# Key norms of the RWKV-7 recurrence: from 512 columns of head sums to 8 columns with tokens on partitions, spread by products with the identity

## The reference, cut to what matters

```python
kk = heads(k * lp["rwkv_k_k"].astype(f32))
kk = kk / jnp.maximum(jnp.sqrt(jnp.sum(kk * kk, axis=-1, keepdims=True)), 1e-12)
...
y, s = wkv_scan(rh, heads(decay), kh, vh, -kk, kk * ah, s0.astype(f32))
```

## Time and profile before

| | us |
|---|---|
| median of 3 runs (1955.46 to 1959.11) | 1958.74 |
| the profiled execution | 1956.71 |
| its span | 1954.9 |
| PE busy in it | 1886.3 (96%) |
| DVE busy | 1355.1 (69%) |
| ACT busy | 872.5 (45%) |
| PE's share of the chain that ended last | 74% |
| DVE's share of that chain | 15% |

### The profile page before, as it was taken

How to read it: one execution, slowest core, us unless ns; L and a number is a source line. 1 busy time by engine, 2 the same in 40 slices (tenths; PEclk the granted TensorE clock), 3 DMA queues, 4 the chain that set the end, 5 groups by cost and what they waited for, 6 DMA issues and landing times.

```text
span 1954.9 us, 53598 instructions
## 1 busy us (share of the span) xinstructions
PE 1886.3 (96%) x22088; PEld 1748.8 (89%) x22088; DVE 1355.1 (69%) x2232; ACT 872.5 (45%) x1710; POOL 72.2 (4%) x143
## 2 busy tenths in 40 slices
PE   7999999998999999999999999999989999999997
PEld 7999888776789999999999998887667999999997
DVE  3485767888646999962265767688886389999423
ACT  4223335554445566552232234545536355666421
POOL 0000000000000111100000000000000001111000
PEclk9999899999999999999999999999999999999999
DMA  6225534244421333233332264432442222332232
GB/s 223 87 86 157 162 110 141 68 113 115 114 93 55 119 109 100 85 98 98 103 134 87 76 189 149 135 120 68 123 134 86 91 97 88 99 108 87 88 97 91
DMA packets 153014, 214.30 MB, mean 110 GB/s; under 512 B 18497, under 2 KB 118338, under 8 KB 151362
## 3 DMA queue, kind: packets, MB, share of 16 engines
q1 hardware_dynamic: 134050, 200.38, 33.0%
q10 hardware_dynamic: 18720, 10.49, 1.8%
HBM read 202.58 MB, written 16.59 MB: 112 GB/s over the span
## 4 chain that ended last, share of the span: by engine, by line
PE 74%; DVE 15%; ACT 4%; issue 3%; DMA 2%; ACTq 1%; SPq 0%; DVEq 0%
PE ps L1110 12%; PE ps L1112 11%; PE ps L1111 11%; PE ps L1646 5%; PE ps L1648 5%; PE ps L1647 5%; PE ps L1500 4%; PE ps L1378 1%; DMA ring<-in_w 1%; PE ps L1471 1%; PE ps L1367 1%; PE ps L1131 1%; PE ps L1464 1%; PE ps L1132 1%; DVE arena L2500 1%
## 5 line engine op out<-in xcount | busy, mean ns | idle before, releaser
L2226 DVE TENSOR_TENSOR ring_lo<-ring,ring_hi 128x1024 fp32r<-128x1024 f32 x84 | 102.9, 1225 | 196.9 <-ACT ring_hi L1703 195.0
L1112 PE MATMUL ps<-hf_hi,ring_lo 128*128 128x260 f32 x704 | 198.9, 283 | 0.0
L1112 PE MATMUL ps<-in_hi,ring_lo 128*128 128x260 f32 x704 | 198.8, 282 | 0.0
L1703 ACT ACTIVATE ring_hi<-ring 128x1024 fp32r<-128x1024 f32 x84 | 88.8, 1058 | 212.1 <-DMA ring<-in_w 209.6
L1112 PE MATMUL ps<-hm_hi,ring_lo 128*128 128x260 f32 x480 | 136.9, 285 | 0.0
L1112 PEld LDWEIGHTS ps<-hf_hi,ring_lo 128*128 128x128 f32 x704 | 132.7, 188 | 0.0
L1112 PEld LDWEIGHTS ps<-in_hi,ring_lo 128*128 128x128 f32 x704 | 132.6, 188 | 0.0
L1110 PE MATMUL ps<-in_hi,ring_hi 128*128 128x260 f32 x448 | 128.8, 287 | 1.7 <-DVE ring_lo L2226 1.7
L1110 PE MATMUL ps<-hf_hi,ring_hi 128*128 128x260 f32 x448 | 127.5, 285 | 0.6 <-issue 0.3
L1111 PE MATMUL ps<-hf_lo,ring_hi 128*128 128x260 f32 x448 | 126.6, 283 | 0.0
L1111 PE MATMUL ps<-in_lo,ring_hi 128*128 128x260 f32 x448 | 126.6, 283 | 0.0
(11 more groups left out here) (543 smaller groups left out, 6116.9 us busy)
## 6 DMA issues: line engine op xcount, KB each, us to landing
ring<-in_w SPq DMA_DIRECT2D x158, 512.0 KB, 3.5
arena<-in_w SPq DMA_DIRECT2D x44, 512.0 KB, 3.5
extra<-in_kv_cmp SPq DMA_DIRECT2D x96, 128.0 KB, 2.3
arena<-in_kv_cmp SPq DMA_DIRECT2D x80, 128.0 KB, 2.7
slot<-in_kv_cmp SPq DMA_DIRECT2D x80, 128.0 KB, 2.4
out_win_old<-in_win SPq DMA_DIRECT2D x16, 511.0 KB, 4.3
slot<-in_k_sel SPq DMA_DIRECT2D x72, 64.0 KB, 2.0
extra<-in_k_sel SPq DMA_DIRECT2D x72, 64.0 KB, 1.9
```

The source lines that it names most:

```text
L1112: last = mmul(out, wl, hi[:, k, cols], start=False, stop=(ci == len(chunks) - 1 and k == k1 - 1))
L1703: A(w_high(l, n), w_place(l, n), ACT.Copy).then_inc(S["w_hi"], 1)
L2226: v.tensor_tensor(w_low(l, n), w_place(l, n), w_high(l, n), SUB).then_inc(S["w_lo"], 1)
```

## The change

The sums are formed the other way round. `kknorm` takes each 128x128 tile of squares as the stationary operand and two columns of `blk` as the moving one, so tokens come out on partitions and the 8 norms of a token in 8 columns. `keymix` on DVE takes the maximum with 1e-24 and the reciprocal on these 128x8 before its own product, `root` on ACT takes the root of 128x8 of the result, and a new PE stage, `kspread`, brings the 8 columns back to channels on partitions: eight products whose stationary operand is one column broadcast to 64 and whose moving operand is the identity, into bank 3. `keys` multiplies from bank 3 and forms `bb`; maximum and reciprocal on 512 columns are gone. `mean` now waits for the next pass's `keys`. The samples' step keeps `bounded` on its 32 columns.

```diff
-PER_SC = {..., "kk1": 2, ...
+PER_SC = {..., "kk1": 3, ...
...
-        put("root", "ACT", 0.72, *here("kknorm"))
-        put("keys", "DVE", 5.42, *here("root"))
+        put("root", "ACT", 0.35, *here("keymix"))
+        put("kspread", "PE", 1.0, *here("root"))
+        put("keys", "DVE", 1.7, *here("kspread"))
...
+        kinv = t1.rearrange("p j t -> p (j t)")[:, 0:2 * RJ]
...
-                        mmul(ps[:, 3, :], blk, t0, start=True, stop=True).then_inc(T["kk1"], 1)
+                        for j in range(RJ):
+                            last = mmul(ps[:, 3, 2 * j:2 * j + 2], t0[:, j, :], blk[:, 0:P:HD], start=True, stop=True)
+                        last.then_inc(T["kk1"], 1)
+                    elif stage == "kspread":
+                        pe.wait_ge(*at_sc("root1", 1))
+                        for j in range(RJ):
+                            for h, r in enumerate(HP):
+                                last = mmul(ps[r, 3, j * SC:(j + 1) * SC], kinv[:, 2 * j + h:2 * j + h + 1].to_broadcast((P, HD)), ident, start=True, stop=True)
+                        last.then_inc(T["kk1"], 1)
...
-                            pe.wait_ge(*at_sc("root1", 1))
...
-                            pe.wait_ge(*at_sc("root1", 2))
+                            pe.wait_ge(*at_sc("prep", 3))
...
                     elif stage == "root":
-                        act.wait_ge(*at_sc("kk1", 1))
-                        o.go(A(t1, b4(3), ACT.Sqrt))
+                        act.wait_ge(kk_rec, l * (LAST_SC + 1) + sc + 1)
+                        o.go(A(kinv, kinv, ACT.Sqrt))
...
                     elif stage == "keymix":
                         dve.wait_ge(*at_sc("kk1", 1))
                         dve.wait_ge(*at_sc("cc_ok", 1))
+                        o.do(v.tensor_scalar(kinv, ps[:, 3, 0:2 * RJ], 1e-24, None, MAX))
+                        o.do(v.reciprocal(kinv, kinv))
+                        dve.sem_inc(kk_rec, 1)
                         o.go(v.tensor_tensor(km, cc, x_sc[:, RJ:2 * RJ, :], MUL))
                     elif stage == "keys":
-                        dve.wait_ge(*at_sc("root1", 1))
-                        bounded(o, kk, t1, aa, bb)
+                        dve.wait_ge(*at_sc("kk1", 2))
+                        o.do(v.tensor_tensor(kk, kk, b4(3), MUL))
+                        o.go(v.scalar_tensor_tensor(bb, aa, 1.0, kk, ADD, MUL))
                         o.tell(T["prep"])
```

More of the change, by code:

```diff
@@ L54 @@
 QR = 32
+LAST_SC = SEQ // SC - 1
 QD = DEC // 2
@@ L184, in constants @@
     return c, np.concatenate([cos, sin], 1)
-PER_SC = {"sq1": 1, "rw_ok": 1, "cc_ok": 1, "rkb": 1, "act1": 2, "lora1": 2, "sig1": 2, "ld_ok": 1, "kk1": 2, "gl_mm": 1, "y_mm": 2, "gg_ok": 1, "rk_ok": 2, "root1": 1, "exp1": 1, "prep": 2,
+PER_SC = {"sq1": 1, "rw_ok": 1, "cc_ok": 1, "rkb": 1, "act1": 2, "lora1": 2, "sig1": 2, "ld_ok": 1, "kk1": 3, "gl_mm": 1, "y_mm": 2, "gg_ok": 1, "rk_ok": 2, "root1": 1, "exp1": 1, "prep": 2,
           "gmm": 4, "gmask": 4, "nmm": 1, "inv_q": LEVELS - 1, "inv_qc": LEVELS - 1,
@@ L417, in warm_thread @@
     return [(("warm", i, "ones"), "PE", 0.9, [att[-2][0]]) for i in range(WARM)]
[L420 to L426, removed]
+ORDER = ("700077897880870901788801788071088787087789907088788008887717180088710817071800889177108091071807170898110827978887828333"
+         "828322778228832728878272782797778827827788338922783828238388712178978217822797772828832771872788282781787889117718888281"
+         "221872897822721787218372289212887227117288727878872878282747878824224872438788828427479888889737322278927328882337878273"
+         "342738288372828712387772287128873727781781789271622178217891722177882788117298727287228122777812782811272282822776827872"
+         "847493242846782824272326982273727367237924232738722742378231971727392371112277682121772728121971712211977262722782611872"
+         "873282292822728827278278288277826298722487286844782282272288299697682477327267277274782329763327287827232797237687227782"
+         "9234772272274272222723727332273722764477874438577874a58488a7a84")
 def merged_order():
@@ L828, in build @@
         gate_in, val_in = x_ok[0:2], x_ok[2:5]
+        kk_rec = ctx.enter_context(nc.semaphore("kk_rec"))
         const_ok = ctx.enter_context(nc.semaphore("const_ok"))
@@ L2473, in rwkv @@
                     elif stage == "rkv":
-                        dve.wait_ge(*at_sc("kk1", 2))
+                        dve.wait_ge(*at_sc("kk1", 3))
                         o.go(v.tensor_tensor(rk, b4(3), y, MUL))
```

## The result

| | before | changed |
|---|---|---|
| median, us | 1958.74 (5 runs, 1955.46 to 1961.10) | 1976.70 (5 runs, 1969.92 to 1979.28) |
| the profiled execution, us | 1956.71 | 1979.28 |
| its span, us | 1954.9 | 1976.2 |
| mean granted clock, of full speed | 0.989 | 0.982 |
| PE busy, us | 1886.3 | 1908.9 |

The changed kernel takes 1.0087 times the time of before, 95% interval [1.0070, 1.0104], or 17 us more. The forecast was 6.3 us more. The direction was right, the size was not, and 1976.7 lies above the range of 1957 to 1970.

A forecast was written before the change was run, and what follows sets the result against it. No engine alone bounds the mixed stretch; the path changes hands between PE and DVE. Passes 0 to 3 sum 0.2 + 1.6 + 0.2 + 4.3 = +6.3 us, giving 1965.0 against the median, range 1957.0 to 1970.0.

The forecast's parts named there:

- DVE's work: Maximum and reciprocal leave keys, two small operations come in: DVE gets 3.4 us less per pass, 27 in all.
- kknorm: PE's norm products in each pass: the eight two-column records take 0.07 us less than before, where PE is the path.
- kspread: PE's new stage in each pass: sixteen records cost 0.88 us, taken from L1485's row.
- Step 2, pass 1: PE alone is the path in pass 1, DVE's saving lies in idle time: +0.8 us, both layers +1.6.
- Step 3, pass 2: In pass 2 DVE's 2.7 us gain turns into its wait for PE; both layers +0.2 us.
- Step 4, pass 3: In pass 3 kspread stands behind solve, delaying keys, mask, sel_bias and sel_new: +2.3 and +2.0 us, both layers +4.3.
- Step 1, pass 0: In pass 0 keys ends 1.5 us earlier but PE is 1.3 later, using up slack; both layers +0.2 us.
- The rival on the clock: Around first-layer pass 0, PE's 1.2 GHz level lasts two more of L1500's groups: +2.2 us, 1967.2; chance 0.08.
- The dense parts: Outside the mixed stretches, the same list runs as before; costed at nothing.
- the dearer spread: Rival: kspread at L1500's rate, 2.18 instead of 0.88 us, adds 5.2 in passes 1 and 3: 1970.2; chance 0.07.
- The rival that DVE's release counts: PE has slack in passes 0 and 2, so DVE's gains are kept: -6.0 us, 1952.7; chance 0.13.
- the rival that pass 3 doesn't lose: sel_k's transfer or ACT is pass 3's real last wait, so only +2.0 us is left, 1960.7; chance 0.17.

The follow-up runs named there:

- e11: Changed kernel with kknorm at 128 moving columns and without kspread, so keys waits only for the root; 1959.0 us, ratio 1.0010 to before.
- e4: Changed kernel without kspread, two-column kknorm kept, keys waiting only for the root; 1966.2 us, ratio 1.0046 to before.
- r_after: The changed kernel again without edit, for a second trace; 1975.1 us, ratio 1.0088 to before.
- r_before: The kernel before again without edit, for a second trace; 1957.2 us, ratio 1.0003.
- e6: Changed kernel with pass 3's kspread moved up on PE from behind solve to behind rhs; 1972.8 us, ratio 1.0080 to before.
- e10: Changed kernel with 128-column kknorm and kspread moved up on PE in passes 0, 1 and 3; 1971.5 us, ratio 1.0069 to before.
- e8: Changed kernel with kknorm's moving operand widened from two columns to 128; 1969.1 us, ratio 1.0066 to before.
- e1: Changed kernel with the old 128x512 product issued ahead of kknorm's two-column products, its result overwritten; 1974.6 us, ratio 1.0083 to before.
- r_after3: The changed kernel once more without edit, for a third trace; 1974.0 us, ratio 1.0087 to before.
- e13: Kernel with the new form and 128-column kknorm in pass 0 alone, passes 1 to 3 old; 1959.0 us, ratio 1.0013 to before.

## Why the prediction was wrong in size

- **DVE's work**, 27 us less: right, 27.6. The small operations take 0.167 and 0.203 (0.2 each forecast).
- **kknorm**, 0.07 less: right at 2.4 GHz (0.98), and missing its main cost, below.
- **kspread**, 0.88: it is 1.02 on the chain, 0.14 more in each place. The Trainium skill's page ("TensorE: Matmul & The Clock Gate", "Back-to-back issue gap") would have had 1.3, an estimate; the measured value lies between it and L1485's row. That row was read where L1485 stands behind L1481, records of the same shape; elsewhere in the same chain (521.25) it took 1.03. A small term.
- **Step 2, pass 1**, +0.8 a layer: right in the first (+0.8). The second has +1.5; the additional 0.7 I can't place.
- **Step 3, pass 2**, +0.1: +0.4 and +0.7. The gain turned into a wait as argued, and kspread's higher price is part of the rest.
- **Step 4, pass 3**, +2.3 and +2.0: right as a mechanism in the first layer and, from `solve` to `sel_new`, in size (+2.5, +2.1): the distance is 5.95 to 6.02 in all three traces of the changed kernel and 3.90 to 4.02 in e11 and e4. The stretch lost +2.3 and +3.4 in r_after. The part that I left out in the second layer is the low clock right behind the stall (1.89 us idle, then 3.4 us at 0.50). There the size is partly luck: e4 and e11 lose as much in that stretch to the transfer, at distances of 7.10 and 5.40.
- **Step 1, pass 0**, +0.1 a layer: this is the step that failed. It lost +3.1 and +3.4, at the low clock, and e4 against e11 shows that the two-column products are what keeps it low, or brings it down again, behind `kknorm` (the first trace of before is +2.9 in the first layer by a longer low stretch of its own, so the single figures are soft). The rival on the clock named the cause and gave it 0.08, but sized it as two groups of L1500 in the first layer only, +2.2 in all; the pair measured 7.2. I had taken the low stretch of the first layer as given and the second layer, at 2.4 GHz in the earlier trace rows, as safe. It wasn't safe: before, PE had fallen there too, for 3.4 us right ahead of `kknorm`.
- **The dense parts**, costed at nothing: the second step that failed, +4.3, +4.0 in the third trace. The list of work was the same. SP's issues were not.
- **The upper end**, 1970.0, was said to take in both upper rivals, but the dearer spread gave 1970.2. It changes nothing here.

In sum for r_after: pass 0 6.5, passes 1 to 3 9.1 (6.1 forecast), the dense part 4.3, and -3.0 in the other two dense stretches, of which 2.0 is r_before's own tail: 17 us. The rival that DVE's release counts falls with e11: with nothing of the new wait left, it wins nothing. Of the rival that pass 3 doesn't lose, the transfer that it named is real: it is as late as DVE in some traces of the changed kernel, and comes next once the stall is taken away (e6, e10, and e4 and e11 in the second layer).

What stays open is why SP's issues take longer. All traces of the changed kernel, of e6, e8 and e10 have it (from the last `ring` issue ahead of the small ones to the next, 5.2 to 6.1 us), and all others have 3.8 to 4.0, e1 among them, though e1 contains the whole change. So it isn't the stages as such. The traces show a part of it. In those six a packet of 16384 bytes of the instruction queue (q8) begins 0.24 to 0.30 us ahead of the first of the small issues, and in e1 0.73 us ahead. In all seven the issue ends 0.37 or 0.38 us after the packet does, and takes 1.01 to 1.34 us (e1 0.56) instead of 0.43. In the eleven other traces no such packet is under way then. So the first issue seems to wait for instructions to be loaded, and where the packet falls depends on the build; this is an inference from the times alone, and it accounts for 0.6 to 0.9 us. Why the later issues, up to 1.46 us each, are long too stays open. Nor was it tried to move the low stretch ahead of pass 0, which before has too, by other means.

## What to carry to other kernels

Turning one wide product into several narrow ones at equal PE time isn't neutral where PE comes out of a low stretch: look for low stretches of the granted clock in the trace before, in every repetition of the place, and price the edit as if each could get longer. Before moving work off a second engine, ask what its next operation waits for; where that is the path's engine, the time saved becomes a wait, and a step added in that engine's order makes it a longer one. A shape with more columns and the same weights cost nearly the same here (0.11 us more per `kknorm`), and is worth trying first.

## What the runs showed of the hardware

- Four products (eight records) with 128x128 weights take 0.98 us on the chain with 2 columns, and with 128 columns 1.09 (e8's `kknorm`, same weights): 64 times the columns cost 0.11 us. The narrow form cost 7.2 us in all (e4 against e11), at a mean clock of 0.9822 instead of 0.9875.
- At 1.2 GHz the two-column form took 1.67 instead of 0.98, though its time hardly depends on its columns; its weight loads took up to 338 ns each instead of 192.
- In pass 3, low stretches followed PE's waits of 1.84 us (e8), 1.89 (r_after), 2.07 (e11) and 2.74 (e4), and followed neither 1.34 and 1.18 (r_before) nor 2.00 (r_after3), 2.19 (r_after) and 2.32 (e13). The length of the wait alone doesn't decide it.
- The same seven small transfer issues on SP took 3.4 us in one build and 5.8 in another, in all three traces of the changed kernel. The first of them ended 0.37 to 0.38 us after a packet of the instruction queue wherever one was under way (seven traces).
